# The second norm of each block-two stage, applied behind PSUM, with the first two units fed k by k

## What is computed

```python
def rmsnorm(x, g):
    xf = x.astype(jnp.float32)
    y = xf * lax.rsqrt(jnp.mean(xf * xf, axis=-1, keepdims=True) + RMS_EPS)
    return (y * g.astype(jnp.float32)).astype(x.dtype)

def second_block(x, ...):
    for layer in range(DEPTH):                       # DEPTH = 2
        h = rmsnorm(x, norm_mix_pre[layer])
        m = attention_mixer(h, ...) if layer % 2 == 0 else recurrent_mixer(h, ...)
        x = x + rmsnorm(m, norm_mix_post[layer])
        h = rmsnorm(x, norm_ffn_pre[layer])
        f = (jax.nn.silu(h @ w_gate) * (h @ w_up)) @ w_down
        x = x + rmsnorm(f, norm_ffn_post[layer])
    return x
```

## Time and profile before

| | us |
|---|---|
| median of three runs | 2956.39 |
| lowest, highest | 2955.84, 2959.55 |
| the profiled execution | 2955.72 |
| its span in the trace | 2953.9 |
| PE busy with matmuls in the span | 2544.5 |
| DVE, ACT, POOL busy | 1406.4, 936.6, 207.9 |

### The profile page before, as it was taken

How to read it: one execution, slowest core, us unless ns; L and a number is a source line. 1 busy time by engine, 2 the same in 40 slices (tenths; PEclk the granted TensorE clock), 3 DMA queues, 4 the chain that set the end, 5 groups by cost and what they waited for, 6 DMA issues and landing times. The chain is left out here.

```text
span 2953.9 us, 47694 instructions
## 1 busy us (share of the span) xinstructions
PE 2544.5 (86%) x19606; PEld 1942.4 (66%) x19606; DVE 1406.4 (48%) x2317; ACT 936.6 (32%) x1510; POOL 207.9 (7%) x347
## 2 busy tenths in 40 slices
PE   5889898958867999886886899889999897899997
PEld 1277677748845766655775566558878565588785
DVE  1145552267764565236675666453332454533423
ACT  0233443211123344321113556342222355422221
POOL 0000000045300000005520000000000000000000
PEclk9989999879978899988998999889999999999998
DMA  9441111100001211110002111123333221233332
GB/s 328 117 71 47 33 32 45 45 2 3 4 22 36 79 36 37 57 39 2 3 4 84 51 57 58 52 62 93 99 89 94 88 64 58 64 92 99 91 92 73
DMA packets 300767, 185.10 MB, mean 63 GB/s; under 512 B 5650, under 2 KB 284708, under 8 KB 300460
## 3 DMA queue, kind: packets, MB, share of 16 engines
q1 hardware_dynamic: 293580, 166.79, 18.9%
q0 software_dynamic: 1808, 5.26, 1.1%
q10 hardware_dynamic: 5200, 10.49, 1.0%
HBM read 177.79 MB, written 4.71 MB: 62 GB/s over the span
## 5 line engine op out<-in xcount | busy, mean ns | idle before, releaser
L244 DVE TENSOR_TENSOR wlo<-wraw,whi 128x1024 fp32r<-128x1024 f32 (+1 forms) x276 | 333.5, 1208 | 602.1 <-ACT whi L237 601.1
L281 PE MATMUL PW<-hhi,whi 128*128 128x512 f32 (+1 forms) x1184 | 448.5, 379 | 64.3 <-DVE hlo L762 39.2
L282 PE MATMUL PW<-hhi,wlo 128*128 128x512 f32 (+1 forms) x1184 | 445.2, 376 | 0.0
L283 PE MATMUL PW<-hlo,whi 128*128 128x512 f32 (+1 forms) x1184 | 444.7, 376 | 0.0
L237 ACT ACTIVATE whi<-wraw 128x1024 fp32r<-128x1024 f32 (+1 forms) x276 | 288.3, 1045 | 315.6 <-PE PW L283 291.2
L281 PEld LDWEIGHTS PW<-hhi,whi 128*128 128x128 f32 x1184 | 226.0, 191 | 114.7 <-issue 49.8
L336 PE MATMUL PW<-hhi,whi 128*128 128x512 f32 (+1 forms) x640 | 244.4, 382 | 23.7 <-DVE hlo L735 18.8
L283 PEld LDWEIGHTS PW<-hlo,whi 128*128 128x128 f32 x1184 | 225.8, 191 | 40.2
L282 PEld LDWEIGHTS PW<-hhi,wlo 128*128 128x128 f32 x1184 | 226.2, 191 | 38.8
L338 PE MATMUL PW<-hlo,whi 128*128 128x512 f32 (+1 forms) x640 | 228.6, 357 | 0.0
L337 PE MATMUL PW<-hhi,wlo 128*128 128x512 f32 (+1 forms) x640 | 228.5, 357 | 0.0
(11 more groups left out here) (376 smaller groups left out, 4319.8 us busy)
## 6 DMA issues: line engine op xcount, KB each, us to landing
wraw<-in_w_in SPq DMA_DIRECT2D x68, 512.0 KB, 3.8
wraw<-in_ffn_w_gate SPq DMA_DIRECT2D x44, 512.0 KB, 3.7
wraw<-in_ffn_w_up SPq DMA_DIRECT2D x44, 512.0 KB, 3.7
wraw<-in_ffn_w_down SPq DMA_DIRECT2D x32, 512.0 KB, 3.7
mod_w<-in_mod_w SPq DMA_DIRECT2D x7, 2048.0 KB, 8.2
wraw<-in_attn_w_in SPq DMA_DIRECT2D x24, 512.0 KB, 3.6
mod_w<-in_mod_w ACTq DMA_DIRECT2D x5, 2048.0 KB, 19.8
wraw<-in_w_out SPq DMA_DIRECT2D x16, 512.0 KB, 3.7
```

The lines of the kernel that those rows point to most:

```text
L244: dve.tensor_tensor(wlo[:, slot, 0:kb, :], wraw[:, slot, 0:kb, :], whi[:, slot, 0:kb, :].bitcast(F32), ALU.subtract).then_inc(S("w_split"), 1)
L281: pe.matmul(acc, whi[:, u % 2, k, :], rhi[:, k0 + k, s0:s1], start=a, stop=False)
L282: pe.matmul(acc, wlo[:, u % 2, k, :], rhi[:, k0 + k, s0:s1], start=False, stop=False)
L283: last_mm = pe.matmul(acc, whi[:, u % 2, k, :], rlo[:, k0 + k, s0:s1], start=False, stop=b)
```

## The change

**What it does.** A new helper `Ramp` replaces `post_norm` and `pre_norm` at the four stage starts. The second root is not applied to h but to each unit's result as it leaves PSUM: h is x by its gain only. So high and low parts of block k can be made as soon as x's block k is new. PE takes units 0 and 1 together, k by k (`pe_ramp`). POOL multiplies the branch by the first root (blocks 1 to 7, DVE block 0), DVE multiplies by the gain and adds to x in one operation. The squares are added in pairs on DVE, so that PE sums four in place of eight. The second root is made behind the last block; every evacuation of these stages is then a DVE product of PSUM and root. The Silu, and all eight Gelus of the mixer, become ACT operations of their own from SBUF. The split of unit 1's weights comes ahead of the first root, that of unit 2's behind the second. The roots lie in columns 512 to 767 of xT, which block two doesn't use.

```diff
+        def pe_ramp(pe, st, ramp, accs, rhs, n):
+            pe.wait_ge(S("w_split"), st["g0"] + 2)
+            for k in range(8):
+                pe.wait_ge(*ramp.ready(k))
+                for u in range(2):
+                    pe.matmul(accs[u], whi[:, u, k, :], rhs[0][:, k, 0:n], start=k == 0, stop=False)
+                    pe.matmul(accs[u], wlo[:, u, k, :], rhs[0][:, k, 0:n], start=False, stop=False)
+                    ins = pe.matmul(accs[u], whi[:, u, k, :], rhs[1][:, k, 0:n], start=False, stop=k == 7)
+                    if k == 7:
+                        ins.then_inc(S("w_used"), 1)
+                if k % 2 and k > 1:
+                    ramp.pe_pair(pe, k // 2 - 1)
+                yield
+            ramp.pe_pair(pe, 3)
+            yield
...
+        class Ramp:
...
+            def pe_pair(self, e, p):
+                e.wait_ge(self.paired.sem, self.paired.at(p + 1))
+                e.matmul(PW[3][:, 0:SEQ], ones, self.sq[:, 2 * p % 4, :], start=p == 0, stop=p == NB // 2 - 1) \
+                 .then_inc(self.summed.sem, 1)
+            def act(self, a, st):
+                a.preload_act_table_set("natural_log_exp_and_others")
+                hi_part(a, 0, st, 1, st["body"][1])
+                a.wait_ge(self.summed1.sem, self.summed1.at(1))
+                inverse_root(a, self.root1, self.work, self.halves(PW[2][:, 0:SEQ]), D, epsc[:, 0:1]).then_inc(self.rooted1.sem, 1)
+                for b in range(NB):
+                    a.wait_ge(self.xnew.sem, self.xnew.at(b + 1))
+                    a.activation(self.into[0][:, b, 0:SEQ], xT[:, b, 0:SEQ], ACT.Identity, scale=self.gpre(b)) \
+                     .then_inc(self.rounded.sem, 1)
+                    if b >= 4 and b % 2 == 0:
+                        a.wait_ge(self.summed.sem, self.summed.at(b // 2 - 1))
+                    a.activation(self.sq[:, b % 4, :], xT[:, b, 0:SEQ], ACT.Square).then_inc(self.squared.sem, 1)
+                a.wait_ge(self.summed.sem, self.summed.at(NB // 2))
+                inverse_root(a, self.rstd, self.work, self.halves(PW[3][:, 0:SEQ]), D, epsc[:, 0:1]).then_inc(self.rooted.sem, 1)
+            def pool(self, g):
+                g.wait_ge(self.rooted1.sem, self.rooted1.at(1))
+                for b in range(1, NB):
+                    if b >= 2:
+                        g.wait_ge(self.taken.sem, self.taken.at(b - 1))
+                    g.tensor_tensor(self.halves(self.tmp[:, b % 2, :]), self.halves(self.m[:, b, 0:SEQ]), self.root1, ALU.mult) \
+                     .then_inc(self.branch.sem, 1)
+            def dve(self, v, st):
+                lo_part(v, 0, st, 1, st["body"][1])
+                v.wait_ge(self.rooted1.sem, self.rooted1.at(1))
+                v.tensor_tensor(self.halves(self.tmp[:, 0, :]), self.halves(self.m[:, 0, 0:SEQ]), self.root1, ALU.mult)
+                v.drain()
+                for b in range(NB):
+                    if b:
+                        v.wait_ge(self.branch.sem, self.branch.at(b))
+                    v.scalar_tensor_tensor(out=xT[:, b, 0:SEQ], in0=self.tmp[:, b % 2, :], scalar=self.gpost(b),
+                                           in1=xT[:, b, 0:SEQ], op0=ALU.mult, op1=ALU.add).then_inc(self.xnew.sem, 1)
+                    v.drain().then_inc(self.taken.sem, 1)
+                    if b:
+                        self.dve_low(v, b - 1)
+                self.dve_low(v, NB - 1)
+                v.wait_ge(self.rooted.sem, self.rooted.at(1))
+            def dve_low(self, v, b):
+                v.wait_ge(self.rounded.sem, self.rounded.at(b + 1))
+                v.scalar_tensor_tensor(out=self.into[1][:, b, 0:SEQ], in0=xT[:, b, 0:SEQ], scalar=self.gpre(b),
+                                       in1=self.into[0][:, b, 0:SEQ].bitcast(F32), op0=ALU.mult, op1=ALU.subtract) \
+                 .then_inc(self.low.sem, 1)
+                if b % 2:
+                    sq = self.sq[:, b % 4, :]
+                    v.wait_ge(self.squared.sem, self.squared.at(b + 1))
+                    v.tensor_tensor(self.sq[:, (b - 1) % 4, :], self.sq[:, (b - 1) % 4, :], sq, ALU.add) \
+                     .then_inc(self.paired.sem, 1)
+            def scale(self, v, dest, acc):
+                return v.tensor_tensor(self.halves(dest), self.halves(acc), self.rstd, ALU.mult)
...
-                        return eng.activation((q, k, vch)[j][:, tr % 2, :], acc, ACT.Copy)
-                    outs.append(("act", ev))
+                        return ramp.scale(eng, (q, k, vch)[j][:, tr % 2, :], acc)
+                    outs.append(("dve", ev))
...
-                return eng.activation(gb[:, 0, :], acc, ACT.Silu)
+                return ramp.scale(eng, gb[:, 0, :], acc)
...
-                eng.tensor_tensor(gb[:, 1, :], gb[:, 0, :], acc, ALU.mult)
+                return ramp.scale(eng, gb[:, 1, :], acc)
+            def act_silu(eng, i, o):
+                if o == 0:
+                    eng.wait_ge(S("evac_done0"), i + (st_gu["o0"] // 2 + 1))
+                    eng.activation(gb[:, 0, :], gb[:, 0, :], ACT.Silu).then_inc(silu.sem, 1)
+            def dve_gated(eng, i, o):
+                if o == 0:
+                    return
+                eng.drain()
+                eng.wait_ge(silu.sem, i + silu.at(1))
+                eng.tensor_tensor(gb[:, 1, :], gb[:, 0, :], gb[:, 1, :], ALU.mult)
...
-                    return eng.activation(gate[:, u - 8, :], acc, ACT.Copy if u < GELU_FROM else ACT.Gelu_apprx_tanh)
-                outs.append(("act", ev))
+                    return ramp.scale(eng, xr[:, u, :] if u < 8 else gate[:, u - 8, :], acc)
+                outs.append(("dve", ev))
```

More of the change, by code:

```diff
@@ L252, in do @@
                         nxt = st["next"]
-                    if nxt is not None:
+                    if nxt is not None and not ("ramp" in st and isinstance(i, int) and i == 0 and u == 0):
                         part(eng, i, st, u + 1, nxt)
@@ L2262, in recurrent @@
                     order += beside.get(8 * u + c, [])
-            order += [("unit", nu), ("gated", 6), ("mix", 6), ("gated", 7), ("mix", 7)]
+            order += [("unit", nu), ("gelu", 7), ("gated", 6), ("mix", 6), ("gated", 7), ("mix", 7)]
             def pe_program(e):
-                for part in before + [norm]:
-                    part["pe"](e)
+                ramp.pe(e)
                 dense = pe_units(e)
@@ L2275, in act_program @@
             def act_program(a):
-                for part in before + [norm]:
-                    part["act"](a)
+                ramp.act(a, st)
                 dense = act_units(a)
@@ L2293, in dve_program @@
             def dve_program(v):
-                for part in before + [norm]:
-                    part["dve"](v)
+                ramp.dve(v, st)
                 dense = dve_units(v)
```

169 lines of the change are left out of this document (104 added, 65 removed).

## The result

The changed kernel takes 2964.8 us (median of six runs, 2961.9 to 2968.4) against 2955.7 us of the kernel before on the same chip: a ratio of 1.003, 95% interval 1.002 to 1.004. It is 9.1 us slower; the forecast was 2966.0, and its chance for a time above 2962.3 was 0.52. The profiled execution took 2961.94 us, the shortest of the six, with a span of 2960.1 us and a granted clock of 0.928.

The account below looks back on a forecast made before the run. The prediction took four stage starts, where PE waits behind DVE, as the bound. Ramps -4.0, clock +8.5 and evacuation +5 gave +9.5 us on 2955.7: 2965.2, as a median 2966; own range 2959 to 2973, whole range 2943 to 2977.

Parts of the forecast that it names:

- The bound: Four stage starts, from first root to unit 2, where DVE sets the pace: 138.0 us in the kernel before.
- Split of unit 1 ahead of the root: At each stage start, ACT splits unit 1's weights before the first root: 1.05 us, four times, 4.2 us in all.
- Turns: In the ramp, DVE operations with two SBUF inputs and POOL alternate: 14.8 and 9.1 add to 23.9 us.
- Behind the last low half: Last sums and second root 5.1 us, then unit 2's weight split 2.5 us; Silu and its table load add in gate-up.
- Clock: PE stands still before unit 2 and starts it at 1.2 GHz: 2.1 us lost, four times, 8.5 us.
- Evacuation: Moving it from ACT to DVE: gate-up 0, attention 2 +2, mixer +3, together +5 us.
- (a): Rival: POOL's products hide beside DVE in the ramp, last low half at about 19 us, total 2946; chance 0.28.
- (c): Rival: DVE's back-to-back operations always go first and POOL runs only while DVE waits: +10, 2976; chance 0.13.
- (b): Rival: DVE and POOL alternate, but clock stays up in two of four gaps and evacuations cost nothing: 2957; chance 0.17.

Follow-up runs that it names:

- before_dve_evac: The kernel before, with attention 2 and the recurrent mixer evacuating all 40 units on DVE and all Gelus run from SBUF: 2959.87 us, ratio 1.0015.
- squares8: The changed kernel with eight places for the squares in place of four, so ACT doesn't wait for PE's sums: 2961.06 us.
- psum_high: The changed kernel with an extra ACT copy of each high half into PSUM, from which DVE makes the low half: 2955.58 us.
- warm: The changed kernel with three (mixers) or five (gate-up stages) float32 products of constants on PE behind the last sum of squares: 2953.49 us.

## Why the prediction was right

The direction and the two costs named for it, the turns and the clock, are what the runs show. The closeness of the sum is partly luck: the stretches give +6.9 us where +9.5 was forecast, and several terms were off in opposite ways.

**The bound.** Right: all that changed lies between the sums and unit 2, and in the turns that the evacuation touches.

**Split of unit 1 ahead of the root.** Forecast 1.05 us at each place, measured 0.94 (3.60 against 2.66 us). In the first gate-up stage of before this stretch took 3.49 us, since PE's sum took 2.07 us there against 1.12 us at the other starts, at a granted clock of 0.51, a row that I hadn't looked at; so the sum is 2.9 and not 3.8. It belongs to the execution and not to the place: in before_dve_evac the fourth start is the long one (3.36 us).

**Turns.** The rule was read from one row, with POOL as the loser. It holds, and here DVE is the loser: 0.75 us become 1.80. The forecast for the last low half was 23.9 us, measured 24.1; but two errors cancel in it. I added all of POOL's 9.1 us, 1.3 for each product. Measured, DVE lost about 1.05 us for each of the seven: five low halves by 1.05, and 2.0 in the first two updates (3.52 us for both), 7.3 in all. And I had the waits for ACT and PE swallowed, while 1.73 us of them stood on top: 14.8 + 7.3 + 1.7 = 23.8. squares8 shows that 1.0 of this can be had. By the Trainium skill (SBUF — State Buffer, "Who interferes with whom") the loser of such a pair is blocked fully, and the order of issue decides which one it is. The traces of after and psum_high agree, with 1.80 us beside 1.27 and 0.75 us with an input in PSUM, but for a little: a row that is 0.75 us long and ends 0.55 us behind POOL had 0.2 us of its work behind it.

**Behind the last low half.** From the last low half to the second root: forecast 5.1 us, measured 4.9; from there to unit 2 2.3 in the mixers (forecast 2.5) and 4.3 in the gate-up stages (4.4). All four places together: 129.0 us, forecast 129.8.

**Clock.** Forecast 8.5 us from two rows on how long the clock stays down, measured 7.5 by the granted clock, 7.6 by the stretches and 11 by the medians. One reading behind it was wrong: 0.58 over 1634 to 1636 us means 0.3 us at full clock and the rest at half, so the clock fell at 1634.3 and not at 1635.2, 2.1 us behind PE's stop and not 2.9. The term rests on how late the clock rises and not on this.

**Evacuation.** Attention 2: forecast 2, measured 2 to 3. Mixer: forecast 3, measured 0 to 2; the step that failed is that each split stands behind one more operation of DVE and is later by it, since PE's waits for the split stayed (6.8 and 8.3 us against 7.4, and 9.1 with unchanged code). Gate-up: forecast 0; the step that failed is the end of the phase. In the turns DVE's extra operation is hidden, as said, but behind the last up unit nothing hides it: 3.18 us against 2.4, and 0.95 us longer at each stage in the stretches of warm against before (231.97 and 231.93 against 231.00). Together 2.5 + 1.9 = 4.4, and forecast 5: a term that was too large and one that was missing cancel.

**The rivals.** (a), POOL hides, is out by the rows of 1.80 us; what it named as the other bound, ACT's squares, was real and came on top. (c), DVE keeps the port, is out: POOL's products keep their 1.27 us but for the first of each ramp, and DVE is the one that stands. (b) is out by its parts in this profile: the clock fell at all four places, and the evacuation had its price. In squares8's profiled execution (2956.8 us, its median 2961.1) the clock did fall at two of the four places only, as (b) had it.

## What to carry to other kernels

Work given to POOL to unload DVE isn't free where DVE's operations beside it have both inputs in SBUF: here 0.69 us taken off DVE cost it 1.05, so doing the product on DVE was 3.1 us faster for each ramp, at 4.8 us more work. Where a stage starts with a chain of short steps, look for what each engine has queued behind the step that ends it: a weight split that could run beside the sums cost 1.4 to 3.5 us at each start, and PE's stop the clock besides. If PE can't be fed, a few products of constants kept its clock here, for about 2 us at each start.
